# Memory keys laid out by feature, table loads of the scalar engine placed earlier, and the pass count read before the last expert pack

## What is computed

```
for each layer i:
  k, v = rmsnorm(mem_prompt, mem_norm[i]) @ w_mem_kv[i]      # 256 memory tokens, 1024 + 1024 columns
  h = rmsnorm(x, norm_mix[i])
  z = h @ w_in                                               # conv mixer (layer 0) or retention (layer 1), and queries
  xa = softmax(q k^T / 16) v   per head                      # prompt on k, v above; samples on cached k, v
  x = x + concat(mix, xa) @ w_out
  h = rmsnorm(x, norm_ffn[i]); top-1 of 4 groups, top-2 of 8 experts in it
  x = x + sum over chosen experts of gate * (silu(h Wg) * (h Wu)) Wd
return rmsnorm(x, final_norm), new states, and the memory keys k and values v of both layers
```

## Time and profile before

| | |
|---|---|
| median of three runs | 1340.07 us (1339.09 to 1340.31) |
| profiled execution, its own time | 1339.78 us |
| its span, first to last instruction | 1337.9 us |
| busy: TensorE matmuls, weight loads | 1204.8 us (90%), 693.8 us (52%) |
| busy: VectorE, ScalarE, GpSimd | 355.2, 153.9, 11.2 us |
| mean granted TensorE clock | 0.955 of full speed |
| transfers | 364.59 MB, 272 GB/s over the span |

### The profile page before, as it was taken

How to read it: one execution, slowest core, us unless ns; L and a number is a source line. 1 busy time by engine, 2 the same in 40 slices (tenths; PEclk the granted TensorE clock), 3 DMA queues, 4 the chain that set the end, 5 groups by cost and what they waited for, 6 DMA issues and landing times.

```text
span 1337.9 us, 13595 instructions
## 1 busy us (share of the span) xinstructions
PE 1204.8 (90%) x5884; PEld 693.8 (52%) x5884; DVE 355.2 (27%) x868; ACT 153.9 (12%) x340; POOL 11.2 (1%) x22
## 2 busy tenths in 40 slices
PE   6999998998998989869999999996999889888785
PEld 3467776776333434236655555563677743332233
DVE  3222213004021304223234342422300233222224
ACT  2000002002110101010201010110200021000001
POOL 0000000000000000000000000000000000000000
PEclk9999999998999999889999999998999869989998
DMA  9743338731599999994216565557954419999991
GB/s 397 302 159 126 126 128 321 313 126 63 216 430 428 421 428 428 427 427 188 79 63 238 218 227 229 216 240 303 425 188 169 176 34 430 427 428 428 428 426 75
DMA packets 27263, 364.59 MB, mean 273 GB/s; under 512 B 3152, under 2 KB 3168, under 8 KB 5056
## 3 DMA queue, kind: packets, MB, share of 16 engines
q1 hardware_dynamic: 23904, 338.99, 62.1%
q10 hardware_dynamic: 1696, 18.88, 3.4%
q0 software_dynamic: 1600, 5.81, 1.1%
HBM read 339.34 MB, written 24.32 MB: 272 GB/s over the span
## 4 chain that ended last, share of the span: by engine, by line
PE 69%; DMA 26%; DVE 2%; ACT 2%; issue 1%; POOL 0%; SPq 0%; DVEq 0%; POOLq 0%; ACTq 0%
DMA ring<-in_gu 24%; PE bank L621 21%; PE bank L429 12%; PE bank L330 8%; PE bank L486 4%; PE bank L706 4%; PE bank L476 2%; PE bank L517 2%; PE bank L316 1%; PE bank L677 1%; PE bank L442 1%; PE bank L385 1%; PE bank L787 1%; PE bank L408 1%; PE bank L768 1%
## 5 line engine op out<-in xcount | busy, mean ns | idle before, releaser
L621 PE MATMUL bank<-hT,ring 128*128 128x288 f32 x1152 | 285.7, 409 | 4.0 <-DVE hT L1077 3.3
L621 PEld LDWEIGHTS bank<-hT,ring 128*128 128x128 f32 x1152 | 218.8, 191 | 73.7 <-issue 13.9
L486 PE MATMUL bank<-ring,arena 128*32 128x512 f32 x1024 | 132.7, 656 | 55.0 <-DMA ring<-in_gu 53.3
L429 PE MATMUL bank<-arena,ring 128*128 128x288 f32 x640 | 155.7, 406 | 1.8 <-DVEq L1141 1.8
L429 PEld LDWEIGHTS bank<-arena,ring 128*128 128x128 f32 x640 | 121.4, 190 | 35.6 <-issue 2.2
L330 PE MATMUL bank<-ring,arena 128*128 128x512 f32 x256 | 111.2, 594 | 3.1 <-DVE arena L1077 3.1
L486 PEld LDWEIGHTS bank<-ring,arena 128*32 128x32 f32 x1024 | 32.5, 115 | 146.8 <-DMA ring<-in_gu 80.2
L476 PE MATMUL bank<-arena 128*128 128x512 f32 (+1 forms) x192 | 102.0, 659 | 2.4 <-DVE arena L1207 1.7
L330 PEld LDWEIGHTS bank<-ring,arena 128*128 128x128 f32 x256 | 48.2, 190 | 63.4 <-issue 61.9
L517 PE MATMUL bank<-arena 128*128 128x288 f32 x256 | 71.4, 427 | 2.1 <-issue 1.7
L476 PEld LDWEIGHTS bank<-arena 128*128 128x128 f32 (+1 forms) x192 | 32.9, 198 | 73.9 <-issue 72.4
(11 more groups left out here) (206 smaller groups left out, 806.1 us busy)
## 6 DMA issues: line engine op xcount, KB each, us to landing
ring<-in_gu SPq DMA_DIRECT2D x64, 2048.0 KB, 24.9
ring<-in_dn SPq DMA_DIRECT2D x32, 2048.0 KB, 17.4
ring<-in_rin SPq DMA_DIRECT2D x14, 2048.0 KB, 13.4
ring<-in_wkv SPq DMA_DIRECT2D x8, 2048.0 KB, 17.4
ring<-in_cin SPq DMA_DIRECT2D x8, 2048.0 KB, 8.7
ring<-in_kc SPq DMA_DIRECT2D x8, 2048.0 KB, 8.6
ring<-in_vc SPq DMA_DIRECT2D x8, 2048.0 KB, 14.0
ring<-in_st SPq DMA_DIRECT2D x8, 2048.0 KB, 14.9
```

The source lines that it names most:

```text
L429: mm = pe.matmul(bank[1 + o % 4][:, 0:T], w[:, k, :], cat[:, k, :], start=(k == 0), stop=(k == kt - 1))
L486: mm = pe.matmul(bank[2][32 * e:32 * e + 32, :], xt[:, k, 32 * e:32 * e + 32], wv[:, e, kk, :], start=(k == 0), stop=(k == KD - 1), skip_g ...
L621: mm = pe.matmul(outs[o], w[:, o, k, :], src[:, k, :], start=(k == 0), stop=(k == KD - 1))
```

## The change

The keys of both layers are computed with features on the partitions: the weights stand still and the memory tokens move, in sixteen matmuls of 256 columns where there were eight of 512. They are copied straight into `KT`, and stored from there in another layout of the output, which the host turns back. `turn_keys`, `keys_turned`, `Ktok` and `keys1` go. Ahead of each norm's squares ScalarE takes the root of one element, after the roots of the two ffn norms and ahead of each attention the exponential of one element (`idle`, one word). The pass count is read before the last pack, and the branch stays where it was. GpSimd reads it before its wait for the last additions.

```
@@ -53,7 +53,6 @@
 VALUES_IN = {2: 2, 4: 3}
-KEYS_IN = {1: (0, 1), 3: (2, 3)}
@@ -178,6 +175,7 @@
+        idle = small[0:1, 62:63]
         nrm = ar(MSO, 576)
@@ -317,28 +315,25 @@
             KV_BANKS = ((0, 1, 2, 3, 4, 5, 6, 7), (4, 7, 0, 1, 4, 7, 4, 7))
-            KT_BANKS = ((0, 1, 2, 3), (4, 7, 4, 7))
-
             def memory_kv(i, j):
...
                 w = v3(landed(pe, (f"kv{i}", c)), KD)
+                if c < 2:
+                    for o in range(2):
+                        f = (2 * mb + o) * P
+                        for k in range(KD):
+                            if i == 0 and j == 0 and o == 0:
+                                pe.wait_ge(S("normed"), k + 1)
+                            mm = pe.matmul(bank[KV_BANKS[i][j]][:, o * NM:(o + 1) * NM], w[:, k, f:f + P],
+                                           src[:, k, :], start=(k == 0), stop=(k == KD - 1), skip_group_check=True)
+                    mm.then_inc(S("kv_sum"), 1)
+                    return
                 for k in range(KD):
-                    if i == 0 and j == 0:
-                        pe.wait_ge(S("normed"), k + 1)
                     mm = pe.matmul(bank[KV_BANKS[i][j]][:, :], src[:, k, mb * P:(mb + 1) * P], w[:, k, :],
...
                 mm.then_inc(S("kv_sum"), 1)
-
-            def turn_keys(i, groups):
-                src = (Ktok, keys1)[i]
-                for g in groups:
-                    for hd in range(2):
-                        for mb in range(2):
-                            mm = pe.transpose(bank[KT_BANKS[i][g]][:, hd * 256 + mb * P:hd * 256 + (mb + 1) * P],
-                                              src[:, mb, (2 * g + hd) * P:(2 * g + hd + 1) * P], C("ident"))
-                    mm.then_inc(S("kt_turned"), 1)
@@ -543,6 +538,9 @@
                 for i in range(PACKS):
+                    if i == PACKS - 1:
+                        pe.wait_ge(S(f"npass{L}"), 1)
+                        more = pe.value_load(npass[0:1, L:L + 1], min_val=0, max_val=PASSES - 1)
                     pe.wait_ge(S("xt_out_a"), PACKS * L + i + 1)
@@ -557,10 +555,6 @@
                         pe.wait_ge(S("values1_out"), j - 2)
-                    if L == 0 and i in KEYS_IN:
-                        pe.wait_ge(S("gt_out"), i)
-                        turn_keys(1, KEYS_IN[i])
-                        pe.wait_ge(S("kt_out_a"), 2 + KEYS_IN[i][1] + 1)
                     pe.wait_ge(S("gated"), PACKS * L + i + 1)
@@ -576,8 +570,6 @@
-                pe.wait_ge(S(f"npass{L}"), 1)
-                more = pe.value_load(npass[0:1, L:L + 1], min_val=0, max_val=PASSES - 1)
                 with pe.If(more > 0):
@@ -633,11 +625,7 @@
                 memory_kv(0, j)
-            pe.wait_ge(S("ktok_out"), 4)
-            turn_keys(0, range(4))
-
-            pe.wait_ge(S("kt_out_a"), 2)
-            pe.wait_ge(S("kt_out_d"), 2)
+            pe.wait_ge(S("kt_out"), 4)
             pe.wait_ge(S("v_out"), 4)
@@ -843,6 +831,7 @@
                     act.wait_ge(S("sumsq"), NORM[name])
+                act.activation(idle, C("eps")[0:1, :], ACT.Sqrt)
                 for k in range(KD):
@@ -851,25 +840,23 @@
                    .then_inc(S("ms_out"), 1)
+                if name in ("ffn0", "ffn1"):
+                    act.activation(idle, C("eps")[0:1, :], ACT.Exp)
...
                     act.wait_ge(S("kv_sum"), j + 1)
-                    act.activation(Ktok[:, j % 2, (j // 2) * 512:(j // 2 + 1) * 512], bank[j][:, :], ACT.Copy) \
-                       .then_inc(S("ktok_out"), 1)
-                for g in (1, 3):
-                    act.wait_ge(S("kt_turned"), g + 1)
-                    act.activation(KT[:, 2 * g:2 * g + 2, :], v3(bank[g][:, :], 2), ACT.Copy) \
-                       .then_inc(S("kt_out_a"), 1)
+                    act.activation(KT[:, 2 * j:2 * j + 2, :], v3(bank[j][:, :], 2), ACT.Copy).then_inc(S("kt_out"), 1)
...
+                act.wait_ge(S("keys_stored0"), 16)
                 for j in range(4):
                     act.wait_ge(S("kv_sum"), 8 + j + 1)
-                    act.activation(keys1[:, j % 2, (j // 2) * 512:(j // 2 + 1) * 512],
-                                   bank[(4, 7, 0, 1)[j]][:, :], ACT.Copy).then_inc(S("kv1_out"), 1)
+                    act.activation(KT[:, 2 * j:2 * j + 2, :], v3(bank[(4, 7, 0, 1)[j]][:, :], 2), ACT.Copy) \
+                       .then_inc(S("kv1_out"), 1)
                 act.wait_ge(S("kv1_out"), 4)
-                act.dma_start(a["out_mk"][1].rearrange("(m p) n -> p m n", p=P), keys1) \
+                act.dma_start(a["out_mk"][1], KT) \
                     .then_inc(S("keys_stored1"), 16)
@@ -893,14 +880,9 @@
-            def keys_turned(groups):
-                for g in groups:
-                    act.wait_ge(S("kt_turned"), 4 + g + 1)
-                    act.activation(KT[:, 2 * g:2 * g + 2, :], v3(bank[(4, 7)[g % 2]][:, :], 2), ACT.Copy) \
-                       .then_inc(S("kt_out_a"), 1)
-
             def attention(i):
                 act.wait_ge(S("normed"), NORM_DONE[f"mix{i}"])
+                act.activation(idle, C("eps")[0:1, :], ACT.Exp)
                 for j in range(9):
@@ -952,14 +934,15 @@
                 for i in range(PACKS):
+                    if i == PACKS - 1:
+                        act.wait_ge(S(f"npass{L}"), 1)
+                        more = act.value_load(npass[0:1, L:L + 1], min_val=0, max_val=PASSES - 1)
                     act.wait_ge(S("gu_sum"), 4 * PACKS * L + 4 * i + 4)
...
                         values_ahead(VALUES_IN[i])
-                    if L == 0 and i in KEYS_IN:
-                        keys_turned(KEYS_IN[i])
                     act.wait_ge(S("gt_turned"), PACKS * L + i + 1)
@@ -968,8 +951,6 @@
                     act.activation(yo[:, 0:512], bank[5][:, :], ACT.Copy).then_inc(S("y_out_a"), 1)
-                act.wait_ge(S(f"npass{L}"), 1)
-                more = act.value_load(npass[0:1, L:L + 1], min_val=0, max_val=PASSES - 1)
                 with act.If(more > 0):
@@ -990,8 +971,6 @@
                 act.wait_ge(S("cin_sum"), 4 * c + 4)
-                if c == 0:
-                    act.wait_ge(S("keys_stored0"), 16)
                 act.activation(qx[:, c, :], bank[4 * (c % 2) + 3][:, 0:T], ACT.Copy).then_inc(S("qx_out0"), 1)
@@ -1083,9 +1062,6 @@
                        .then_inc(S("v_out"), 1)
-                for g in (0, 2):
-                    dve.wait_ge(S("kt_turned"), g + 1)
-                    dve.tensor_copy(KT[:, 2 * g:2 * g + 2, :], v3(bank[g][:, :], 2)).then_inc(S("kt_out_d"), 1)
@@ -1253,6 +1229,9 @@
                 for i in range(PACKS):
+                    if i == PACKS - 1:
+                        dve.wait_ge(S(f"npass{L}"), 1)
+                        more = dve.value_load(npass[0:1, L:L + 1], min_val=0, max_val=PASSES - 1)
                     dve.wait_ge(S("tanh"), PACKS * L + i + 1)
@@ -1272,7 +1251,6 @@
-                more = dve.value_load(npass[0:1, L:L + 1], min_val=0, max_val=PASSES - 1)
                 with dve.If(more > 0):
@@ -1382,7 +1360,6 @@
             experts(0)
-            dve.wait_ge(S("keys_stored1"), 16)
             norm("mix1", xT, ((hT, "mix1"),), T)
@@ -1475,8 +1452,8 @@
-                pool.wait_ge(S("ktok_out"), 4)
-                pool.dma_start(a["out_mk"][0].rearrange("(m p) n -> p m n", p=P), Ktok).then_inc(S("keys_stored0"), 16)
+                pool.wait_ge(S("kt_out"), 4)
+                pool.dma_start(a["out_mk"][0], KT).then_inc(S("keys_stored0"), 16)
                 pool.wait_ge(S("v_out"), 4)
@@ -1487,9 +1464,9 @@
-                pool.wait_ge(S("y_added"), KD * PACKS * L + KD * PACKS)
                 pool.wait_ge(S(f"npass{L}"), 1)
                 more = pool.value_load(npass[0:1, L:L + 1], min_val=0, max_val=PASSES - 1)
+                pool.wait_ge(S("y_added"), KD * PACKS * L + KD * PACKS)
                 with pool.If(more > 0):
@@ -1527,7 +1504,7 @@
 OUTS = {"out_y": (P, KD, T), "out_cvp": (P, 8, 2), "out_cvs": (P, 8, 16), "out_rp": (H, P, 2, DV),
-        "out_rs": (2 * H, P, SLOT), "out_mk": (2, NM, D), "out_mv": (2, NM, D)}
+        "out_rs": (2 * H, P, SLOT), "out_mk": (2, P, KD, NM), "out_mv": (2, NM, D)}
@@ -1635,7 +1612,7 @@
     rs = r["out_rs"].reshape(H, 2, P, 4, 2, DV).transpose(1, 3, 0, 4, 2, 5).reshape(1, NB, H, 256, DV)
-    mk = r["out_mk"].reshape(2, 1, NM, H, 256)
+    mk = r["out_mk"].transpose(0, 3, 2, 1).reshape(2, 1, NM, H, 256)
     mv = r["out_mv"].reshape(2, 1, NM, H, 256)
```

More of the change, by code:

```diff
@@ L149, in build @@
         hm0 = v3(ar(CATO + 2048, KD * NM), KD)
-        Ktok = v3(ar(PHO, 2048), 2)
-        keys1 = v3(hT_[:, 0:2048], 2)
         qx = v3(ar(PHO, 8 * T), 8)
```

## The result

| | before | changed |
|---|---|---|
| median | 1340.12 us (1339.09 to 1340.31, 4 runs) | 1319.16 us (1314.62 to 1319.66, 4 runs) |
| ratio | | 0.9838 (95% interval 0.9815 to 0.9860) |
| profiled execution, span | 1339.78, 1337.9 us | 1319.31, 1317.5 us |
| mean granted TensorE clock | 0.955 | 0.962 |

The change is worth 21 us, where 6 were forecast.

A forecast was written before the change was run, and what follows sets the result against it. TensorE holds 69% of the chain of waits, transfers bound the experts. Terms 0.15 − 1.6 − 2.4 − 0.2 − 0.6 − 1.4 = −6.0 us from 1339.78 gave 1333.8, as median 1334.1; range 1331.3 to 1336.8.

The forecast's parts named there:

- The branch stays where it is, so only 1.4 goes.: Before the sum over features, both layers: reading the count early saves 1.4 us; the branch's 6.12 and 3.63 us stay.
- the stall goes with the load: Rival at the pass-count branch: the count's load causes the stall, so 7.6 us go instead of 1.4; 1327.9 us, 3%.
- Attention(0), 2.4: Layer 0's attention: an exponential ahead removes the table load and a fall of TensorE's clock, minus 2.4 us.
- The rival with 0.9: Rival in layer 0's attention: TensorE's clock falls all the same, so only 0.9 us goes; 1335.6 us, 14%.
- Keys, 1.6: Gap behind layer 0's last values job: transposes and ScalarE's copy go, VectorE's values copy is late next; minus 1.6 us.
- Keys the other way, nothing: Key jobs in both layers: 32 records of 256 columns take as long as 16 of 512, weight loads hidden; nothing.
- The rival of the weight loads: Rival at the 256 key records, both layers: a quarter of each weight load exposed, plus 12.2 us, 1346.3 us; 3%.
- Norms, routing, start: Table loads moved: ffn norms minus 0.2 us, layer 1's routing minus 0.6; one-element root at the start plus 0.15.
- Packs 1 and 3, nothing: Experts: removing transposes of about 1.8 us each in these packs gains nothing, since transfers cover them.
- Count, 1.4: Pass count read before the last pack: its loads, 0.8 and 0.6 us in the two layers, are hidden; minus 1.4 us.

The follow-up runs named there:

- e2: The changed kernel with the pass count read after the last pack again, right before the branch; 1318.76 us, 0.9855 of the kernel before.
- e3: The kernel before with 48 already-met waits added to TensorE's program in packs 4 to 7 of layer 0; 1327.68 us, 0.9913.
- e4: The changed kernel with 64 added waits, both branches 256 instructions further on than in the kernel before; 1326.72 us, 0.9911.
- e8: The changed kernel with 16 added waits, both branches 208 instructions further on than in the kernel before; 1322.05 us in one run.
- e12: The changed kernel with 32 added waits, both branches 224 instructions further on than in the kernel before; 1330.61 us in one run.
- e1: The kernel before with only the pass count read before the last pack, on all engines; 1337.57 us, 0.9978.
- e10: The changed kernel itself, measured once more in the same rounds as the kernel before; 1318.31 us, 0.9848.
- e5: The kernel before with 96 added waits in TensorE's program, nothing else changed; 1321.86 us, 0.9859.
- e9: The kernel before with 192 added waits, branches placed as in the changed kernel, none of its edits; 1324.01 us, 0.9879.
- e6: The kernel before with only the key edit, count and table loads as before; 1323.32 us, 0.9853.
- e7: The kernel before with only the one-element roots and exponentials, TensorE's program unchanged; 1334.41 us, 0.9944.
- e11: The changed kernel with idle multiplications where TensorE waits, plus 160 added waits in layer 1's experts; 1316.89 us, 0.9835.

## Why the prediction was wrong

**The branch.** The failed step is "The branch stays where it is, so only 1.4 goes." It stayed in the order of the program, but not in its place: the key edit, costed at nothing for its time, puts 192 instructions ahead of it, and TensorE no longer has to wait at it for a block of its program. The branches account for 12.0 us: from the end of the spread to the end of the sum e2, with the count late, has 4.6 and 4.3 us where the kernel before has 11.9 and 9.0. Of that 9.1 is the stall itself, 3.0 the sum at a halved clock behind it. The Trainium skill's rule ("Runtime: NRT & Kernel Launch", "Instruction fetch mechanics") was the right one, and was read only half: it says that the stall hangs on whether the target is in the window, which is a question of place. The packets of the trace and e3, e4, e8 and e12 agree with it. The Trainium skill's "Advanced Engine Details and Errata", "ISA Cache", gives lines of 16 KB or 256 instructions; the packets here are of that size, and so is the unit that the runs show. The rival nearest in time, "the stall goes with the load" (1327.9, 3%), had a wrong cause: e1.

**Attention(0), 2.4.** Mis-sized: 1.5 on average, 1.0 without a fall of the clock. The two profiles of before and after differ by just 2.40 (21.50 and 19.10), but that is the luck of the execution that was profiled. The comparison of two attentions in one trace took for a part of the kernel a fall that happens in two profiles of six. The rival with 0.9 had nearly the size, but not the reason: the clock does not fall with the load gone; most times it does not fall with it there either.

**Keys, 1.6.** Right: the gap is 0.83 for 2.43, and VectorE's copy of the last values is what is late. **Keys the other way, nothing.** Right: 128 records take 27.86 us in e4 and e10 and 29.26 in the change, 64 long ones 27.70 in the kernel before, e5 and e9, and 29.23 in e1 and e3; e6 has 30.84 and e7, with the old form, 30.67. The three lengths come with either form, so they are the clock at the start (1.00, 0.95 and 0.89 granted on average from 16 to 48 us); the form itself costs 0.03 to 0.2. The rival of the weight loads is out.

**Norms, routing, start.** Right: the root now follows the sum, which ends at 301.27 + 1.25, by 0.02 us and not 0.12; 0.12 between ranks and reading for 0.73; 0.1 for 0.15. **Packs 1 and 3, nothing.** From the first gate product of layer 0 to its last group of 16 it is 217.7 us before and 216.9 after, 215.8 in e1 with the transposes: no gain beyond what runs differ by. **Count, 1.4.** Right for the branch that stalls (e1); without the stall it is 1.1 (e2).

**The sum again.** Forecast −6.0, plus 0.9 for attention(0), minus 12.0 for the branches: −17.1 of −21.0. Of the rest, 1.7 is the first `rin` chunk and 1.5 the first pack of layer 1, 7.11 where it took 8.56. Those two durations nearly go with the group: 17.3 to 17.5 and 8.5 to 8.8 us in all seven kernels that lack one of the edits to keys and tables (before, e1, e3, e5, e6, e7, e9), 15.7 to 15.8 and 7.11 in the change, e2, e10 and e11. But of the changed kernels with added waits e4 has 15.76 and 8.80, e8 17.71 and 7.11, e12 18.30 and 8.73, so they don't hang on one cause, and what in the edits moves the clock there is open. What the edits are worth without the branch is the change against e9 and e5: 3 to 6 us, with overlapping intervals, so it is an estimate and not shown.

The two profiles alone add up otherwise, for they hold what differs from run to run: 2.2 us lost by the start of the value jobs (48.96 for 46.77), then won 1.6 at the keys, 2.4 in attention(0), 8.1 and 5.1 from the last spreads to the ends of the sums with the count, 1.7 in the `rin` chunk, 0.5 from there to the first gate product of layer 1, 1.5 in its first pack and 1.8 between that and the last spread; that is the 20.4, but for rounding.

**The range.** It took the four times of one session (1339.1 to 1340.3) for the spread. Over all sessions the kernel before gave 1335.2 to 1344.6, the changed one 1313.5 to 1326.3.

## What to carry to other kernels

Where a program branches, look at the sequencer's own rows (COMPARE_BRANCH), not only at "issue" in the chain. Any edit that changes the number of instructions ahead of a taken branch can win or lose several us at it, whatever the edit does; so count them in the forecast, look where the instruction packets fall, and before crediting an edit with a gain pad the kernel before to the same place. And a difference of two stretches in one profile holds that execution's clock; price the load by itself until a second profile agrees.

## What the runs showed of the hardware

A taken branch of TensorE over 300 instructions costs 0.32 to 0.38 us or 3.3 to 6.5, by its place modulo 256 instructions, and once 2.11 between the two (e3). It takes 6.0 to 6.5 in layer 0, where transfers fill the queues at 0.99 and more, and 3.3 to 3.7 in layer 1, where they are idle. TensorE's program comes in packets of 16384 bytes, 256 instructions each; one takes 0.9 to 1.4 us at these branches, and a TensorE that waits for it goes on 1.2 to 1.5 us after its end. A target shortly ahead of a block's end moves the stall into the code behind the branch (1.92 and 3.89 us in layer 0, 0.95 in layer 1). The same branches on ScalarE and VectorE took 0.05 to 0.07 us. A wait that is already met takes TensorE's sequencer 51 ns.
